# Last down product in other banks, output in three parts, router weights standing, modulation in one piece, squares first

## The chip, the cores and the metric

One core of a Trainium2 chip runs the whole program. The metric is device microseconds; less is better. TensorE (PE) multiplies, VectorE (DVE) and ScalarE (ACT) do elementwise work, SyncE (SP) issues nearly all DMA. TensorE's clock has two levels, 1.2 and 2.4 GHz; views give the granted one as a share of the higher.

## The reference, cut to what matters

Two transformer blocks, 256 tokens by 1024 channels, all in float32. The first has two layers, each with modulation from a conditioning vector `c`, a mixer of three attention kinds, and a feed-forward part, dense in layer 0 and a mixture of eight experts in layer 1.

```python
c_act = jax.nn.silu(c)
for layer in range(2):
    mod = c_act @ ada_w[layer] + ada_b[layer]
    sh1, sc1, g1, sh2, sc2, g2 = split(mod, 6)
    h = rms_norm(x, norm_mix[layer]) * (1.0 + sc1) + sh1
    x = x + g1 * mixer(h, ...)                 # begins with h @ w_in
    h = rms_norm(x, norm_ffn[layer]) * (1.0 + sc2) + sh2
    y = swiglu(h, ...) if layer == 0 else moe(h, ...)
    x = x + g2 * y
# moe: logits = h @ w_router (1024x8); top 2; softmax of the two; each expert's swiglu, weighted
# second block:
h = rms_norm(x, norm1_g); proj = h @ w_in_2    # z, xbc (4096 columns), dt, q, k, v, gates
x = x + merged(ssd, attention) @ w_out
u = causal_dwconv(rms_norm(x, norm2_g) @ w_up, ffn_conv_w, ffn_conv_b)
x = x + (silu(u_gate) * u_val) @ w_down        # 5632 columns up, 2816 rows down
```

## The kernel before, in words

All weights are packed on the host in one stream in the order of use, in slots of up to 2048 columns (1 MB). `plan()` lists the slots. SyncE loads them one by one into a ring of four (`load_to`); a slot's place is free when its last user (`last_use`) is done. A slot is one or two chunks of at most 1024 columns. Each chunk is split for TensorE: ScalarE copies the rounded high part to `whi` (`Scalar.split_to`, line 386), VectorE writes what remains to `wlo` (`Vector.split_to`, line 340). There are four pairs of buffers (`NS`), so ScalarE can be four chunks ahead of TensorE. A product of two split numbers is three matmuls (`mm3`, line 238). Transposes go through line 251. Each engine runs its own program written out in order (`tensor_program`, `scalar_program`, `vector_program`, `sync_program`) and waits on counters of the others' finished work; within an engine nothing is reordered, so a `split_to` put ahead of something makes it wait for that chunk.

*Start.* The first 2048 columns of layer 0's modulation (shift and scale of the first norm) come in four quarters of 512, each in two slots. For a quarter, TensorE multiplies half the rows on one partition (`pe_mods`), VectorE sums the other half (`dve_mods`), and TensorE turns both into columns with narrow matmuls (`pe_mods_turn`). The norm's factors `rs` are broadcast along the tokens (`pe_along`), ScalarE copies that (`act_root`), VectorE scales the transposed `x` block by block, ScalarE adds the shift and rounds to `hT`, VectorE makes `hTl` (`dve_mod_t`, `act_mod_t`; eight blocks, with weight splits put between them by `split_between`). Before, quarters 0 and 1 (in plan order the first halves of shift and scale) are followed by blocks 0 to 3 and half of the first projection `inA0`, and quarters 2 and 3 (`pe_second_half`, called at its third chunk) by the rest.

*Routing* (`pe_routing`, 1744). For each of eight blocks k, token columns of `hT` and `hTl` are the stationary operand and 8 router columns the moving one: six matmuls per block. Between them the blocks are turned back to rows (4 transposes each) for the later choice of tokens. The broadcast of the output gate `g3` (16 fp32 records) comes ahead of the ranks, which need VectorE's choice of the two best (`sel`), and the picks (`pe_pick`) need the ranks and `place`.

*Between the blocks.* After the last expert a branch skips the code for an overfull expert (`when_over`). ScalarE then splits the first two chunks of `xbc` (`a.split_to(... + 2)` in `squares`) and squares the rows of `x` (`act_squares`, `act_last_squares`); from the sums come `rs` and the norm, as above. `pe_cols` multiplies the first two blocks of `xbc` together, k by k, as the norm's blocks come.

*End.* `pe_second_ffn` makes 44 blocks of the up product in banks 0 to 3 of PSUM in turn, each read by the convolution on ScalarE and VectorE, then the down product in banks 0 to 3 (two token tiles by two column halves), in 11 slots. `pe_down` takes all four banks ahead of its first matmul. `dve_down` adds the result to `x` in four pieces, column half 0 first; the output is stored by one DMA after the last.

Of the kernel before, what the change touches and what calls it, by code (L numbers as in the profile page):

```python
# [15 lines left out]
KT = D // 128  # L16
# [69 lines left out]
def plan():  # L86
    p = ada(0, 0, 512) + ada(0, 1024, 1536)
    for l in range(2):
# [442 lines left out]
def pe_start(K, pe):  # L531

    pe_mods(K, pe, 0)
    pe_mods(K, pe, 1)
    pe_mods_turn(K, pe, 0)
    pe_mods_turn(K, pe, 1)
    pe_turn(K, pe, "nm0", lambda j, i: K.x[:, i, 128 * j:128 * j + 128], KT, "v")
    pe_along(K, pe, "nm0")
    pe_mods(K, pe, 2)


def pe_second_half(K, pe):

    pe_mods_turn(K, pe, 2)
    pe_mods(K, pe, 3)
    pe_mods_turn(K, pe, 3)
# [16 lines left out]
def dve_start(K, v):  # L563
# [34 lines left out]


# [159 lines left out]
def dve_mod_t(K, v, s, scale, shift=None, j0=0, j1=KT):  # L759
# [9 lines left out]
    for j in range(j0, j1):  # L769
# [469 lines left out]
def pe_mixer(K, pe, l):  # L1239
# [472 lines left out]
def dve_down(K, v, s, parts, gate, norm):  # L1712

    v.split_to(min(parts[-1] + NS - 1, K.fence(parts[-1])))
    for half in range(2):
        if half and norm:
            dve_eps(K, v, norm)
        for i in range(2):
# [5 lines left out]
            else:  # L1724
                v.tt(xs, K.ps[2 * i + half][:, :], xs, ALU.add, key=(s, "y", i, half))
# [18 lines left out]
def pe_routing(K, pe):  # L1744

    pe.take(0)
    block = ready(K, pe, "nf1")
    for k in range(KT):
        block(k)
        o = slice(8 * k, 8 * k + 8)  # L1750
        for i in range(2):
            pe.mm3(K.ps[0][:, 8 * i:8 * i + 8], hrows(K)(k, i), (K.rout[:, 0, o], K.rout[:, 1, o]), k == 0 and i == 0, k == KT - 1,
                   done="logits" if k == KT - 1 and i else None)
        for j in (k - 1, k) if k % 2 else ():
            for part, src in enumerate((K.hT, K.hTl)):
                for i in range(2):
                    b = BACK[part][i]
                    if j % 4 == 0:
                        pe.take(b)
                    pe.tr(K.ps[b][:, 128 * (j % 4):128 * (j % 4) + 128], src[:, j, 128 * i:128 * i + 128].bitcast(F32),  # L1760
# [1302 lines left out]
```

## Time and profile before

| | us |
|---|---|
| median of 3 runs | 2177.68 (2173.34 to 2182.85) |
| profiled execution, device time | 2185.45 |
| its span | 2183.7 |
| ScalarE busy | 1329.7 (61%) |
| DMA engines | 497.18 MB, mean 228 GB/s |
| mean granted clock of TensorE | 0.946 |

The span runs from the first to the last instruction. The order in it is: start and mixer 0 to 229, dense part, mixer 1 to 593, routing to 625, experts to 1423, second block to the end. A time in a row is counted from the span's start; `[a <-b]` says that the engine was idle for a and that b ended it. In a window's row each engine has its busy time and the number of its instructions, then follow the granted clock, the share of time that the DMA engines were busy, and their rate.

### The profile page before, as it was taken

The page shows a single profiled execution, that of the slowest core. Times are in us where ns is not written, and L with a number is a line of the kernel's source. Part 1 is how long each engine was busy: PE and PEld are TensorE (multiplying, and loading weights), DVE is VectorE, ACT ScalarE, POOL GpSimd, SP SyncE. Part 2 cuts the span into 40 slices and gives each one's busy share as a digit, 9 for nine tenths or more (in the row PEclk, how much of TensorE's full clock was granted, in tenths as well). Part 3 has the DMA queues.
Part 4 walks back from the last instruction along what each step waited for, and adds up shares of the span by engine and source line. Part 5 has one row for each costly group of instructions (what it writes and reads, how often), then busy time and mean ns, then how long its engine had stood idle before and what let it go on. Part 6 is the DMA issues. An engine that isn't in the chain of part 4 may idle for free. (4 is left out here: it accounts for less than half of the span.)

```text
span 2183.7 us, 28021 instructions
## 1 busy us (share of the span) xinstructions
PE 2012.0 (92%) x11093; PEld 1731.4 (79%) x11093; DVE 1671.3 (77%) x2155; ACT 1329.7 (61%) x1968; POOL 0.2 (0%) x4
## 2 busy tenths in 40 slices
PE   7878999987899999999999999979999988889999
PEld 4667778876788888888888887769877878878987
DVE  4877888677669989998998999768655655567873
ACT  2564543357568777787877786657556544536652
POOL 0000000000000000000000000000000000000000
PEclk8886999999889999999999999989999989889999
DMA  7615688741249989998998998655314532224542
GB/s 272 232 54 209 245 315 325 282 150 39 97 163 368 360 337 360 360 365 326 363 365 331 357 370 317 246 184 180 137 44 154 198 112 97 97 97 143 186 163 107
DMA packets 70089, 497.18 MB, mean 228 GB/s; under 512 B 8000, under 2 KB 8256, under 8 KB 10688
## 3 DMA queue, kind: packets, MB, share of 16 engines
q1 hardware_dynamic: 69664, 494.28, 61.6%
q8 instruction: 89, 1.46, 0.3%
q10 hardware_dynamic: 288, 1.05, 0.1%
q14 instruction: 48, 0.39, 0.1%
HBM read 494.25 MB, written 1.05 MB: 227 GB/s over the span
## 5 line engine op out<-in xcount | busy, mean ns | idle before, releaser
L340 DVE TENSOR_TENSOR wlo<-ring,whi 128x1024 fp32r<-128x1024 f32 (+1 forms) x845 | 1016.7, 1216 | 292.5 <-ACT whi L386 274.5
L386 ACT ACTIVATE whi<-ring 128x1024 fp32r<-128x1024 f32 (+1 forms) x845 | 886.2, 1054 | 525.9 <-PE ps L238 455.7
L238 PE MATMUL ps<-whi,hT 128*128 128x256 f32 (+2 forms) x944 | 325.2, 344 | 27.6 <-ACT wa L366 4.7
L238 PE MATMUL ps<-wlo,hT 128*128 128x256 f32 (+2 forms) x944 | 319.9, 339 | 0.0
L238 PE MATMUL ps<-whi,hTl 128*128 128x256 f32 (+2 forms) x944 | 319.4, 338 | 0.0
L238 PE MATMUL ps<-whi,xg 128*128 128x512 f32 (+1 forms) x768 | 290.5, 378 | 5.4 <-DVE wlo L340 5.2
L238 PE MATMUL ps<-whi,xgl 128*128 128x512 f32 (+1 forms) x768 | 286.6, 373 | 0.0
L238 PE MATMUL ps<-wlo,xg 128*128 128x512 f32 (+1 forms) x768 | 286.4, 373 | 0.0
L238 PEld LDWEIGHTS ps<-whi,hT 128*128 128x128 f32 x944 | 187.8, 199 | 52.4 <-issue 6.7
L238 PE MATMUL ps<-whi,hf 128*128 128x512 f32 x528 | 210.1, 398 | 11.2 <-DVE wlo L340 4.9
L238 PE MATMUL ps<-wlo,hf 128*128 128x512 f32 x528 | 207.6, 393 | 0.0
L238 PEld LDWEIGHTS ps<-whi,hTl 128*128 128x128 f32 x944 | 187.0, 198 | 17.6
L238 PEld LDWEIGHTS ps<-wlo,hT 128*128 128x128 f32 x944 | 187.4, 199 | 16.8
L238 PE MATMUL ps<-hT,whi 128*128 128x256 f32 (+1 forms) x616 | 176.3, 286 | 6.0 <-DVE hTl L287 4.0
L238 PE MATMUL ps<-hTl,whi 128*128 128x256 f32 (+1 forms) x616 | 175.6, 285 | 0.0
L238 PE MATMUL ps<-hT,wlo 128*128 128x256 f32 (+1 forms) x616 | 174.8, 284 | 0.0
L238 PEld LDWEIGHTS ps<-whi,xg 128*128 128x128 f32 x768 | 145.3, 189 | 31.2 <-DVE wlo L340 6.3
L238 PEld LDWEIGHTS ps<-whi,xgl 128*128 128x128 f32 x768 | 145.2, 189 | 25.9
L238 PEld LDWEIGHTS ps<-wlo,xg 128*128 128x128 f32 x768 | 145.4, 189 | 24.6
L238 PE MATMUL ps<-whi,hf1l 128*128 128x512 f32 x352 | 137.6, 391 | 0.0
L238 PEld LDWEIGHTS ps<-whi,hf 128*128 128x128 f32 x528 | 100.2, 190 | 32.5 <-DVE wlo L340 5.8
L238 PEld LDWEIGHTS ps<-hT,whi 128*128 128x128 f32 (+1 forms) x616 | 117.1, 190 | 7.0 <-ACT hT L366 4.8
(283 smaller groups left out, 2644.9 us busy)
## 6 DMA issues: line engine op xcount, KB each, us to landing
ring<-in_wstream SPq DMA_DIRECT2D x462, 1024.0 KB, 5.0
ring<-in_wstream SPq DMA_DIRECT2D x4, 832.0 KB, 6.2
ring<-in_wstream SPq DMA_DIRECT2D x6, 256.0 KB, 2.7
cst<-in_cst SPq DMA_DIRECT2D x1, 1028.0 KB, 7.6
x<-in_x SPq DMA_DIRECT2D x1, 1024.0 KB, 13.6
work<-in_bias ACTq DMA_DIRECT2D x2, 512.0 KB, 5.2
ring<-in_wstream SPq DMA_DIRECT2D x2, 512.0 KB, 3.9
out_x<-x SPq DMA_DIRECT2D x1, 1024.0 KB, 4.1
```

The source lines that it names most:

```text
L238: i = self.e.matmul(out, lhsT, rhs, start=start, stop=stop, skip_group_check=True)
L340: i = self.e.tensor_tensor(K.wlo[:, q % NS, 0:cols], src, hi.bitcast(F32), ALU.subtract)
L386: i = self.e.activation(K.whi[:, q % NS, 0:cols], K.ring[:, m % RING, at:at + cols], ACT.Copy)
```

## The change

The plan has the eight modulation slots first. The four quarters, with their turns and the transposes of `x`, are done in one run, the quarters in the order of their columns; the scale and all eight blocks of the norm follow, then the first projection without a break. In the routing the 8 router columns are stationary and 256 tokens move (three matmuls per block), the 8 rows of logits are copied by ScalarE and turned by two small transposes; the gate's second half is broadcast after the ranks. The splits ahead of the squares of `n1` are gone; chunks 1, 2 and 4 of `xbc` are split between the norm's blocks 2, 4 and 6. The last down product uses banks 4 to 7. The output goes in three DMAs, each behind its own addition.

```diff
 def plan():
-    p = ada(0, 0, 512) + ada(0, 1024, 1536)
+    p = ada(0, 0, 2048)
...
-                if (l, n, at) == (0, 0, 0):
-                    p += ada(0, 512, 1024) + ada(0, 1536, 2048)
...
 def pe_start(K, pe):
     pe_mods(K, pe, 0)
     pe_mods(K, pe, 1)
     pe_mods_turn(K, pe, 0)
+    pe_mods(K, pe, 2)
     pe_mods_turn(K, pe, 1)
     pe_turn(K, pe, "nm0", lambda j, i: K.x[:, i, 128 * j:128 * j + 128], KT, "v")
+    pe_mods(K, pe, 3)
+    pe_mods_turn(K, pe, 2)
     pe_along(K, pe, "nm0")
-    pe_mods(K, pe, 2)
-def pe_second_half(K, pe):
-    pe_mods_turn(K, pe, 2)
-    pe_mods(K, pe, 3)
     pe_mods_turn(K, pe, 3)
...
 def dve_start(K, v):
...
     dve_eps(K, v, "nm0")
+    dve_root(K, v, "nm0")
+    dve_mods(K, v, 2)
     dve_mods_turn(K, v, 1)
-    dve_root(K, v, "nm0")
-    v.split_to(1)
-    dve_mod_scale(K, v, 0, 0, "nm0", 0, 4)
-    dve_mod_t(K, v, "nm0", K.sc, shift_of(K, 0, 0), 0, 4)
-    dve_mods(K, v, 2)
     dve_mods(K, v, 3)
     dve_mods_turn(K, v, 2)
+    v.split_to(1)
     dve_mods_turn(K, v, 3)
-    dve_mod_scale(K, v, 0, 0, "nm0", 4, 8)
-    dve_mod_t(K, v, "nm0", K.sc, shift_of(K, 0, 0), 4, 8)
...
+BETWEEN = {"nm0": ("inA0", {2: 2, 4: 3, 6: 4}), "nf0": ("ffng", {4: 3, 6: 4}), "nm1": ("inA1", {4: 3, 6: 4}), "n1": ("xbc", {2: 1, 4: 2, 6: 4}),
+           "n2": ("up2", {4: 3, 6: 4})}
 def split_between(K, x, s, j):
-    stage = {"nm0": "inA0", "nf0": "ffng", "nm1": "inA1", "n1": "xbc", "n2": "up2"}.get(s)
-    if j == 2 and s == "nm0":
-        x.split_to(K.parts[stage][0] + 2)
-    if j in (4, 6) and stage:
-        x.split_to(K.parts[stage][0] + 1 + j // 2)
+    stage, parts = BETWEEN.get(s, (None, {}))
+    if j in parts:
+        x.split_to(K.parts[stage][0] + parts[j])
...
 def pe_routing(K, pe):
+    def back(j):
...
     for k in range(KT):
         block(k)
         o = slice(8 * k, 8 * k + 8)
-        for i in range(2):
-            pe.mm3(K.ps[0][:, 8 * i:8 * i + 8], hrows(K)(k, i), (K.rout[:, 0, o], K.rout[:, 1, o]), k == 0 and i == 0, k == KT - 1,
-                   done="logits" if k == KT - 1 and i else None)
-        for j in (k - 1, k) if k % 2 else ():
...
+        pe.mm3(K.ps[0][0:8, 0:256], (K.rout[:, 0, o], K.rout[:, 1, o]), (K.hT[:, k, :], K.hTl[:, k, :]), k == 0, k == KT - 1,
+               done="logit rows" if k == KT - 1 else None)
+        if k:
+            back(k - 1)
+    pe.wait_ge(K.act, "logit rows")
+    for i in range(2):
+        pe.tr(K.ps[0][:, 256 + 8 * i:264 + 8 * i], K.modrow[0:8, 0, 128 * i:128 * i + 128], done="logits" if i else None)
     pe.given(0, (K.dve, "logits"))
-    pe_broadcast(K, pe, "g3", (6, 7))
+    back(KT - 1)
+    pe_broadcast(K, pe, "g3", (6, 7), (0,))
...
     pe.given(2, (K.dve, "count"))
+    pe_broadcast(K, pe, "g3", (6, 7), (1,))
 def act_routing(K, a):
...
     for half in range(2):
+        if half:
+            a.wait_ge(K.pe, "logit rows")
+            a.act(K.modrow[0:8, 0, 0:256], K.ps[0][0:8, 0:256], ACT.Copy, key="logit rows", own=False)
...
     def squares(way):
         by = ("x", 7) if way else ("e", 7)
-        a.split_to(K.parts["xbc"][0] + 2)
...
 def pe_second_ffn(K, pe):
-    pe_down(K, pe, "f2", "down2", lambda k, i: pair(K.hf, k, i), 2, (0, 1, 2, 3), lambda k: ("f2", "lo", k))
+    pe_down(K, pe, "f2", "down2", lambda k, i: pair(K.hf, k, i), 2, (4, 5, 6, 7), lambda k: ("f2", "lo", k))
...
     dve_eps(K, v, "n1")
-    v.split_to(K.parts["xbc"][0] + 1)
     dve_root(K, v, "n1")
-    v.split_to(K.parts["xbc"][0] + 2)
     dve_mod_t(K, v, "n1", K.col("n1", 0, 8))
...
-    sp.wait_ge(K.dve, "end")
+    sp.wait_ge(K.dve, ("f2", "y", 1, 0))
     if sp.e is not None:
-        sp.e.dma_start(out, K.x[:, :, :]).then_inc(K.s_out.sem, 16)
-    sp.wait_ge(K.s_out, 16)
+        sp.e.dma_start(out[:, :, 0:512], K.x[:, :, 0:512]).then_inc(K.s_out.sem, 16)
+    for i in range(2):
+        sp.wait_ge(K.dve, ("f2", "y", i, 1))
+        if sp.e is not None:
+            sp.e.dma_start(out[:, i, 512:1024], K.x[:, i, 512:1024]).then_inc(K.s_out.sem, 16)
+    sp.wait_ge(K.s_out, 48)
```

## Rows read from the trace of the kernel before

**Rows 1.** the page's parts 1 and 5: busy us, count; a group's busy, mean ns

```profile
PE 2012.0 (92%) x11093; PEld 1731.4 (79%) x11093; DVE 1671.3 (77%) x2155; ACT 1329.7 (61%) x1968; POOL 0.2 (0%) x4
...
L340 DVE TENSOR_TENSOR wlo<-ring,whi 128x1024 fp32r<-128x1024 f32 (+1 forms) x845 | 1016.7, 1216 | 292.5 <-ACT whi L386 274.5
```

**Rows 2.** what the loading queue waited for: us in total, times, longest

```profile
SPq L415 <- DVE wlo L340: 1775.5, 419, 55.0
```

**Rows 3.** timeline ahead of the last down product: start us, us, engine, operation

```profile
2111.20 0.28 PE L238 MATMUL ps<-hT,wlo 128*128 128x256 f32 x1
...
2114.76 1.00 DVE L294 SCALAR_TENSOR_TENSOR ffn_w<-ps,cols,ffn_w 128x255 f32<-128x255 f32 x2
...
2116.01 0.77 PE L238 MATMUL ps<-whi,hf 128*128 128x512 f32 x1 [4.54 <-DVE ffn_w L294]
```

**Rows 4.** windows of the down product (engines' busy us, clock, DMA share, GB/s)

```profile
2116.00:2121.00 5.00, 4.99 (x12) 3.94 (x13) 0.71 (x2) 0.42 (x1) 0.00 (x0) 0.51 0.46 188
...
2121.10:2126.10 5.00, 5.00 (x23) 4.13 (x22) 2.17 (x2) 2.12 (x2) 0.00 (x0) 1.00 0.00 0
```

**Rows 5.** timeline of the store, SyncE's queue

```profile
2179.19 0.40 SPq L2758 DMA_DIRECT2D out_x<-x  x1
```

**Rows 6.** DMA issues: count, KB each, median us to landing

```profile
ring<-in_wstream SPq DMA_DIRECT2D x6, 256.0 KB, 2.7
...
out_x<-x SPq DMA_DIRECT2D x1, 1024.0 KB, 4.1
```

**Rows 7.** windows: routing on TensorE, and dense 256-column products at full clock

```profile
599.20:614.40 15.20, 15.20 (x73) 15.20 (x74) 5.06 (x13) 5.62 (x12) 0.00 (x0) 0.50 0.01 1
...
1448.00:1468.00 20.00, 20.00 (x169) 20.00 (x168) 17.45 (x29) 15.18 (x25) 0.00 (x0) 1.00 0.47 159
```

**Rows 8.** timeline of the routing: first read of the logits, ranks, picks

```profile
614.54 0.17 DVE L308 COPY rt<-ps 128x16 f32<-128x16 f32 x1 [10.09 <-PE ps L238]
...
619.20 0.70 PE L238 MATMUL ps<-sel,steps 128*128 128x8 f32 x5
...
621.05 0.72 PE L238 MATMUL ps<-place,rows_hi 128*128 128x256 f32 x4 [1.15 <-DVE count L308]
```

**Rows 9.** windows of a stretch with nothing but transposes on TensorE, and the next

```profile
1547.50:1550.60 3.10, 3.04 (x14) 2.67 (x15) 1.66 (x2) 1.09 (x3) 0.00 (x0) 0.50 0.31 61
...
1550.60:1552.00 1.40, 1.28 (x9) 0.89 (x8) 0.69 (x1) 0.60 (x1) 0.00 (x0) 0.89 1.03 433
```

**Rows 10.** timeline between the experts and the second block's first projection

```profile
1422.09 1.61 DVE L294 SCALAR_TENSOR_TENSOR x<-ps,rt,x 128x512 f32<-128x512 f32 x2 [1.28 <-PE ps L238]
...
1428.77 2.00 ACT L386 ACTIVATE whi<-ring 128x1024 fp32r<-128x1024 f32 x2 [18.63 <-DMA ring<-in_wstream]
...
1436.37 1.19 PE L238 MATMUL ps<-cst,rs 128*128 128x128 f32 x4 [8.78 <-DVE rs L294]
...
1447.12 0.36 PE L238 MATMUL ps<-hT,whi 128*128 128x256 f32 x1 [0.58 <-ACT hT L366]
```

**Rows 11.** windows of the start: turns, transposes, a quarter, the projection's second half

```profile
19.10:21.70 2.60, 2.55 (x16) 2.36 (x16) 0.91 (x2) 2.56 (x5) 0.00 (x0) 1.00 1.00 417
...
21.90:26.10 4.20, 4.15 (x17) 4.05 (x18) 0.17 (x1) 1.89 (x7) 0.00 (x0) 0.50 1.01 419
...
26.00:29.40 3.40, 3.40 (x17) 3.40 (x18) 0.97 (x6) 0.00 (x0) 0.00 (x0) 0.50 0.24 101
...
44.60:50.40 5.80, 5.80 (x9) 0.80 (x9) 0.00 (x0) 0.58 (x1) 0.00 (x0) 0.62 0.63 255
...
57.60:64.60 7.00, 7.00 (x25) 6.82 (x26) 5.29 (x8) 3.67 (x5) 0.00 (x0) 0.64 0.58 207
```

**Rows 12.** timeline of VectorE at the start: sums, second half of the scale loop

```profile
41.76 2.33 DVE L294 SCALAR_TENSOR_TENSOR gate<-ring,cact,gate 128x512 f32<-128x512 f32 x3
...
55.24 0.48 DVE L294 SCALAR_TENSOR_TENSOR aux<-ps,sc,cbm 128x256 f32<-128x256 f32 x1
...
60.41 0.49 DVE L294 SCALAR_TENSOR_TENSOR hTl<-aux,mod,hT 128x256 fp32r<-128x256 f32 x1 [0.19 <-ACT hT L368]
```

More of the change, by code:

```diff
@@ L746, in act_mod_t, with dve_mod_scale @@
             a.act(K.hT[:, j, :], K.rtmp4[:, j % 4, :], ACT.Identity, bias=shift[:, j:j + 1], key=(s, "hi", j), own=False)
-def dve_mod_scale(K, v, layer, which, gain, j0=0, j1=KT):
-    at = 8 * which + 8
-    v.stt(K.sc[:, j0:j1], K.mod[:, layer, at + j0:at + j1], 1.0, K.col(gain, j0, j1 - j0), ALU.add, ALU.mult)
+def dve_mod_scale(K, v, layer, which, gain):
+    v.stt(K.sc[:, :], K.mod[:, layer, 8 * which + 8:8 * which + 16], 1.0, K.col(gain, 0, 8), ALU.add, ALU.mult)
     v.last()
@@ L756, in shift_of, with dve_mod_t @@
     return K.mod[:, layer, 8 * which:8 * which + 8]
-def dve_mod_t(K, v, s, scale, shift=None, j0=0, j1=KT):
+def dve_mod_t(K, v, s, scale, shift=None):
     def low(j):
@@ L768, in dve_mod_t @@
     v.wait_ge(K.act, (s, "along"))
-    for j in range(j0, j1):
+    for j in range(KT):
         v.wait_ge(K.pe, (s, "t", j // 2 * 2))
@@ L774, in dve_mod_t @@
               key=(s, "v", j), own=False)
-        if j > j0:
+        if j:
             low(j - 1)
         split_between(K, v, s, j)
-    low(j1 - 1)
+    low(KT - 1)
 def pe_rows(K, pe, key, lhs, kt, banks=(0, 1, 2, 3), by=(("dve", 0), ("dve", 1)), block=None, at_part=None):
@@ L910, in dve_mods_turn, with pe_broadcast @@
 def dve_mods_turn(K, v, u):
-    at = (0, 8, 4, 12)[u]
     v.wait_ge(K.pe, ("modturn", u))
-    v.tt(K.mod[:, 0, at:at + 4], K.ps[COLUMN][:, 0:4], K.col("ab0", at, 4), ALU.add, key=("mods", u))
-def pe_broadcast(K, pe, s, banks):
-    for half in range(2):
+    v.tt(K.mod[:, 0, 4 * u:4 * u + 4], K.ps[COLUMN][:, 0:4], K.col("ab0", 4 * u, 4), ALU.add, key=("mods", u))
+def pe_broadcast(K, pe, s, banks, halves=(0, 1)):
+    for half in halves:
         b = banks[half]
@@ L1251, in values @@
         pe_values(K, pe, s, x, js[x])
-    pe_rows(K, pe, f"inA{l}", hrows(K), KT, by=COPIES, block=ready(K, pe, f"nm{l}"),
-            at_part=None if l else lambda n: pe_second_half(K, pe) if n == 2 else None)
+    pe_rows(K, pe, f"inA{l}", hrows(K), KT, by=COPIES, block=ready(K, pe, f"nm{l}"))
     pe_rows(K, pe, f"inD{l}", hrows(K), KT, by=COPIES, banks=BANKS_D)
@@ L1709, in dve_dense, with dve_down @@
     dve_down(K, v, "ff", parts, True, "nm1")
-def dve_down(K, v, s, parts, gate, norm):
+def dve_down(K, v, s, parts, gate, norm, bank=0):
     v.split_to(min(parts[-1] + NS - 1, K.fence(parts[-1])))
@@ L1724, in dve_down @@
             else:
-                v.tt(xs, K.ps[2 * i + half][:, :], xs, ALU.add, key=(s, "y", i, half))
+                v.tt(xs, K.ps[bank + 2 * i + half][:, :], xs, ALU.add, key=(s, "y", i, half))
 def act_down(K, a, parts, norm):
@@ L1744, in pe_routing @@
 def pe_routing(K, pe):
+    def back(j):
+        for part, src in enumerate((K.hT, K.hTl)):
+            for i in range(2):
+                b = BACK[part][i]
+                if j % 4 == 0:
+                    pe.take(b)
+                pe.tr(K.ps[b][:, 128 * (j % 4):128 * (j % 4) + 128], src[:, j, 128 * i:128 * i + 128].bitcast(F32),
+                      done=("back", j // 4, part, i) if j % 4 == 3 else None)
+                if j % 4 == 3:
+                    pe.given(b, (K.act, ("rows", j // 4, part, i)))
     pe.take(0)
@@ L1750, in pe_routing @@
         o = slice(8 * k, 8 * k + 8)
-        for i in range(2):
-            pe.mm3(K.ps[0][:, 8 * i:8 * i + 8], hrows(K)(k, i), (K.rout[:, 0, o], K.rout[:, 1, o]), k == 0 and i == 0, k == KT - 1,
-                   done="logits" if k == KT - 1 and i else None)
-        for j in (k - 1, k) if k % 2 else ():
[L1755 to L1760, printed above, removed]
-                          done=("back", j // 4, part, i) if j % 4 == 3 else None)
-                    if j % 4 == 3:
-                        pe.given(b, (K.act, ("rows", j // 4, part, i)))
+        pe.mm3(K.ps[0][0:8, 0:256], (K.rout[:, 0, o], K.rout[:, 1, o]), (K.hT[:, k, :], K.hTl[:, k, :]), k == 0, k == KT - 1,
[5 more added lines that the diff above has]
+        pe.tr(K.ps[0][:, 256 + 8 * i:264 + 8 * i], K.modrow[0:8, 0, 128 * i:128 * i + 128], done="logits" if i else None)
     pe.given(0, (K.dve, "logits"))
-    pe_broadcast(K, pe, "g3", (6, 7))
+    back(KT - 1)
+    pe_broadcast(K, pe, "g3", (6, 7), (0,))
     pe.take(2)
@@ L1800, in dve_routing @@
     v.wait_ge(K.pe, "logits")
-    v.copy(lg, K.ps[0][:, 0:16].rearrange("p (i e) -> p i e", i=2), key="logits")
+    v.copy(lg, K.ps[0][:, 256:272].rearrange("p (i e) -> p i e", i=2), key="logits")
     eidx = K.cst("eidx").unsqueeze(1).to_broadcast([128, 2, 8])
```

8 lines of the change are left out of this document (6 added, 2 removed).

## The prediction

> **What bounds the kernel now.** I read the page's busy shares first: TensorE is busy 92% of the span, VectorE's low split is the largest group beside it, 845 times 1.22 us [rows 1]. Then the loading queue's waits: its ring issue waits 419 times, 1775.5 us in all, for VectorE's low split, that is for room in the ring, so the loads are ahead of their use and DMA isn't the bound [rows 2]. What is left to win is where PE stands still or runs at half its clock: the start, the routing, the step from the experts to the second block, and the end. The timelines and windows of those places carry the rest.
>
> Profiled execution: span 2183.7, device time 2185.45 us; that is 7.8 above the median of the runs, 2177.68. I make the sum as a difference and take it off both.
>
> **1. Last down product in banks 4 to 7.** The up product's last matmul starts at 2111.20; the down product starts at 2116.01, after VectorE's last convolution taps (2114.76 + 1.00) free banks 0 to 3 [rows 3]. In the stop the clock fell: from 2116 12 matmuls take 5.00 us at 0.51 clock, later 22 to 23 take as much at 1.00 [rows 4], so 12 x (0.417 - 0.227) = 2.3 us more. Banks 4 to 7 hold nothing read after the last norm. The first chunk needs rows 0 of the hidden state, long split, and its weights: the splits run four chunks ahead, and the four that are ready give PE 4 x 12 x 0.227 = 10.9 us, to 2122.3. The fifth needs PE's release of the first (2114.1) and the last hidden rows off ScalarE and VectorE (about 2117), hence is split by about 2119: nothing is late next. Gain 4.81 - 0.24 (two steps of the old stream) + 2.3 = 6.9 us, bounds 6.3 and 7.2.
>
> **2. Output in three parts.** Now the store is issued at 2179.19, when the last add is done, and takes 4.1 us for 1 MB [rows 5, 6]. The last 256 KB now go alone; the first 512 KB start some 4.5 us and the second part 1.4 us earlier. The nearest row for 256 KB is a ring load's 2.7 us [rows 6]. Gain 4.1 - 2.7 = 1.4; bounds 0.5 (the parts queue up) and 2. SP's two more waits hold up nothing but the stores.
> The Trainium skill ("DMA: Bandwidth & Descriptors", Latency) puts a fixed cost of about 2 us on any transfer; by it nothing under 2 us is left of the 4.1, which agrees with the row.
>
> **3. Routing.** Now 48 matmuls of 8 columns and 28 transposes run from 599.2, 73 of them in 15.2 us at clock 0.50: 0.208 each, since each loads 128 columns of weights [rows 7]. The logits are read at 614.54, PE ranks at 619.20, picks at 621.05 [rows 8]. After: 24 matmuls with 8 weight columns and 256 moving ones (0.118 each at full clock, 169 in 20 us [rows 7], so 0.21 at half), and 28 transposes (the last four come behind the logits): 52 in all.
> All at half clock: 52 x 0.213 = 11.1, logit rows at 610.3; ScalarE's copy and two small transposes 1.3, logits at 611.6 instead of 614.54. From there to the ranks it was 4.66 but VectorE's chain is only 2.7 of it (half of the gate broadcast is now behind the ranks): ranks about 614.4, picks 1.85 later plus 0.4 for the second half broadcast: 616.6, gain 4.4.
> But this stream is full: every operation streams 256 cycles back to back, and such streams do raise the clock in this trace (below). It starts low; I let it rise about 5 us in, as at the start of the down product above (2116 to 2121 [rows 4]). Then 24 operations at 0.213 and 28 at 0.12: logit rows 607.7, ranks 612.1, picks 614.1, gain 7.0. PE then waits for VectorE about 1.5 us with little to do, which may cost the clock again: half of the 32 picks' difference, 1 us. I take 6; bounds 2 (half clock, and the picks too) and 8.5. Behind PE's new wait for ScalarE's copy stand only the two transposes, the last back-turn and the broadcast.
> The Trainium skill ("TensorE: Matmul & The Clock Gate", Part 4) says transposes don't count as busy for the clock gate, which would speak against me: 28 of the 52 are such. But here a stretch of nothing but fp32 transposes from 1547.5 runs at 0.50 and the clock is up in the next window, 0.89 [rows 9]. The trace disagrees; I go by it.
>
> **4. Squares first.** Now ScalarE splits two chunks ahead of the squares, and those wait 18.63 us for a load that lands at 1428.77, while x is final at 1423.7 (1422.09 + 1.61). So the rows' broadcast comes at 1436.37 [rows 10]. After: squares of the first half at 1419.5, of the second to 1425; root by 1426.5; broadcast when the transposes end, 1427.7; factors on VectorE from about 1429.8, 8 us earlier. Not all stays: both splits of the first two chunks now stand inside that loop (VectorE 4 x 1.22 in place of 2 x 1.22), and PE needs both chunks for its first product. Walking the loop (0.4 per VectorE step, 1.0 and 1.22 per split [rows 1, 10]) gives the second split at 1436.5 and the last low part at 1442.0. PE: 48 products from 1436.6, 5 us at half clock, then 0.12 each: ends 1444.6. Before, the last six of them started at 1447.12 [rows 10] and ended at 1447.9. Gain 3.2; bounds 0.5 (VectorE passes its branch late) and 5.
>
> **5. Modulation in one piece.** Now PE does two quarters of the modulation and half of the first projection, then two more quarters and the projection's second half, 57.6 to 64.6 [rows 11]. After, one run: quarter 2, turn 1, transposes of x, quarter 3, turn 2, broadcast, turn 3. A quarter took 5.8 at clock 0.62, so 3.6 at full and, as my estimate, 6.8 at half; a turn 2.6 at full or 4.2 at half, the transposes 3.4 at half [rows 11]. The loads run at 417 GB/s to about 27 [rows 11], 2.5 us a slot, so the slot of PE's third quarter is in at about 21.7, when PE is free; its 0.2 MB more than the w_in slot that stood there costs nothing more. From 21.7: quarter 5.3 (starts low), turn 2.9, transposes 3.4, quarter 4.6, turn 2.6, broadcast 0.5, turn 2.6: 43.6. VectorE's sums (2.33 + 0.5 = 2.8 each [rows 12]) run beside these. The w_in slots wait for ring places freed at 27 and land by 33, hidden; so do the other constants, queued behind one more slot. The scale loop then starts about 45, where now its second half starts at 55.24 and ends at 60.9 [rows 12]: 5.7 with two splits, so 2 x 5.7 - 1.0 = 10.4 for the whole. PE starts two steps in, at 46.9, and its 48 matmuls, 5 us at half clock (15) and 33 at 0.187, end 11.3 later: 58.2 against 64.6. (In the second half 25 took 7.0 at 0.64 [rows 11], 0.28 each, the mean of 0.345 and 0.187.) That is 6.4, and 5 is my value, one handover more being likely. Bounds: all at half clock, 21.7 + 6.8 + 4.2 + 3.4 + 6.8 + 4.2 + 1.1 + 4.2 = 52.4, end 65.6, a loss of 1; all at full, gain 8.
> The following projection's slots were waited for by none, and stay so.
>
> **Sum:** 6.9 + 1.4 + 6 + 3.2 + 5 = 22.5 us: 2163.0 for the profiled execution, 2155.2 for the median.
>
> **The rivals.**
> A, routing stays low: if turns don't raise the clock, step 3 gives 2 to 4.4, say 2.5: 2158.7. For it: the clock stood at 0.50 through 15 us of busy PE [rows 7]. Against: rows 9; and what ran then had 8 columns. 12%.
> B, the front's gains are given back: in the experts the stream of weights is nearly as fast as the loads can go, and if it were the bound, only steps 1, 2 and 4 (11.5) count: 2166.2. Against: the ring is full nearly always [rows 2]. 9%.
> C, squares first brings nothing, because VectorE comes out of its branch late, and the splits are in the loop: 19.3 left, 2158.4. 8%.
> D, slower than before: the start becomes a chain in which nothing overlaps. Per quarter 6.8 + 2.8 sums + 0.9 copy + 4.2 turn + 0.4, twice, and transposes and broadcast 4.5, splits 2, loop 10.4, then PE's 16.6 at half clock: 21.7 + 30.2 + 33.5 = 85.4, 21 us later than 64.6, against 17.5 won elsewhere: 2181. It decides from a first projection ending past 82 us. Against: VectorE's sums ran beside PE's quarters before. 4%.
> The forecast itself: 67%.
>
> **How the numbers follow.** Likeliest 2155.2. All lower bounds give a gain of 8.3, all upper ones 30.7; both at once are unlikely, and the runs of before spread by about 5 us each way. Range 2145 to 2168, which takes in A, B and C. About 0.5% (10.9 us) is what a measurement of this kernel can tell from no change: faster means under 2166.8. Nearly all of the forecast, A and C, and half of B lie there: 0.87; within 0.10; slower 0.03.
>
> **What would show it.** Down product: no stop between up2 and it, clock 1.00 through. Store: last transfer about 2.7 us. Routing: the first logits copy by 610 and the clock up before the picks. Squares: ScalarE's squares ahead of its splits, the row broadcast near 1428 (less what was won before). Start: first projection in one piece, over by about 58. Wrong would be: a DMA wait of PE's in the experts, a turn of the start at half clock throughout, a gap ahead of the fifth down chunk.

## The result, and the profile after

The changed kernel took 2156.38 us (median of 4 runs, 2151.98 to 2157.23) against 2176.48 for the kernel before beside it (4 runs, 2173.34 to 2182.85): ratio 0.9904, 95% interval 0.9882 to 0.9926. 2155.2 was forecast, with 2145 to 2168 as the range. Two more measurements of the same change, 5 rounds each, gave 0.9888 and 0.9889. The profiled execution after has a span of 2154.6 us, and 2156.47 with what lies around it, which is its median; the one before had 2183.7 and 2185.45, 9.0 above its median, so this pair of traces differs by 29.1 where the medians differ by 20.1. Every reading below is therefore taken inside a stretch, from one event to the next, and not from absolute times.

The page after, part 1, and its group of low splits; they answer to [rows 1]:

```profile
PE 2001.1 (93%) x11071; PEld 1718.9 (80%) x11071; DVE 1670.7 (78%) x2154; ACT 1329.6 (62%) x1969; POOL 0.2 (0%) x4
...
L338 DVE TENSOR_TENSOR wlo<-ring,whi 128x1024 fp32r<-128x1024 f32 (+1 forms) x845 | 1016.3, 1216 | 283.3 <-ACT whi L384 265.4
```

TensorE's work is nearly the same, 10.9 us less busy: what went are stops and time at the low clock. (L338 is the low split, L384 the high one, L236 a matmul, L249 a transpose; the kernel before has them two lines later.)

**The down product.** Timeline of TensorE where up ends and down begins, against [rows 3], and the windows against [rows 4] (busy us of PE, PEld, DVE, ACT, POOL, then the clock, DMA share, GB/s):

```profile
2091.28 0.28 PE L236 MATMUL ps<-hT,wlo 128*128 128x256 f32 x1
2091.41 0.39 PE L236 MATMUL ps<-whi,hf 128*128 128x512 f32 x1
```

```profile
2092.00:2097.00 5.00, 5.00 (x24) 4.11 (x23) 3.90 (x8) 2.60 (x5) 0.00 (x0) 1.00 0.48 151
2097.00:2102.00 5.00, 5.00 (x24) 4.14 (x23) 3.40 (x4) 2.50 (x3) 0.00 (x0) 1.00 0.48 152
```

The stop of 4.54 us is gone and the clock stays at 1.00, where it was 0.51; 24 matmuls run in 5 us from the first. No gap came ahead of the fifth chunk. From the start of the last up matmul to the start of the last add it was 67.27 us and is 60.20.

**The store.** Timeline of VectorE's last adds, of SyncE's queue, and the page's part on DMA issues, against [rows 5, 6]:

```profile
2151.49 0.69 DVE L285 TENSOR_TENSOR x<-ps,x 128x512 f32<-128x512 f32 x1 [0.67 <-PE ps L236]
```

```profile
2147.49 0.41 SPq L2757 DMA_DIRECT2D out_x<-x  x1
2150.84 1.69 SPq L2761 DMA_DIRECT2D out_x<-x  x2
```

```profile
out_x<-x SPq DMA_DIRECT2D x1, 512.0 KB, 2.8
...
out_x<-x SPq DMA_DIRECT2D x2, 256.0 KB, 2.0
```

The last 256 KB land in 2.0 us where 1 MB took 4.1; from the end of the last add to the end of the span it is 2.46 instead of 4.49. The Trainium skill ("DMA: Bandwidth & Descriptors", Latency and other measured facts) calls about 2 us the fixed part of a transfer. These stores lie under that: 2.0 us is the whole time of 256 KB, and as 1 MB took 4.1 and 512 KB 2.8, the part that does not grow with the size is, as an estimate from these two, 2.8 - 1.3 = 1.5 us.

**The routing.** Timeline of TensorE from the first router matmul, then windows, against [rows 7, 8]:

```profile
591.02 0.37 PE L236 MATMUL ps<-hT,rout 128*8 128x256 f32 x1 [2.15 <-DVE hTl L292]
...
598.87 0.33 PE L249 MATMUL ps<-cst,hTl 128*128 128x128 f32 x1 [0.16 <-ACT lowl L364]
...
600.80 0.28 PE L249 MATMUL ps<-cst,modrow 8*128 8x8 f32 x2
...
603.91 0.72 PE L236 MATMUL ps<-sel,steps 128*128 128x8 f32 x5 [1.34 <-DVE sel L285]
604.49 1.14 PE L236 MATMUL ps<-aux,cst 128*128 128x128 f32 x8
605.78 1.02 PE L236 MATMUL ps<-place,rows_hi 128*128 128x256 f32 x4 [0.16 <-DVE count L306]
```

```profile
591.00:594.00 3.00, 2.98 (x14) 2.05 (x15) 3.00 (x9) 1.86 (x4) 0.00 (x0) 0.50 0.00 0
594.00:597.00 3.00, 3.00 (x21) 2.62 (x20) 2.08 (x6) 1.84 (x6) 0.00 (x0) 0.71 0.00 0
597.00:600.00 3.00, 2.42 (x16) 1.43 (x15) 0.00 (x0) 1.81 (x4) 0.00 (x0) 1.00 0.00 0
600.00:603.00 3.00, 2.54 (x21) 2.06 (x19) 1.53 (x9) 1.99 (x5) 0.00 (x0) 1.00 0.03 8
603.00:606.00 3.00, 1.94 (x15) 1.77 (x16) 1.89 (x10) 0.45 (x1) 0.00 (x0) 1.00 0.00 0
606.00:609.00 3.00, 3.00 (x16) 3.00 (x16) 0.69 (x1) 1.05 (x2) 0.00 (x0) 0.50 0.00 0
```

The clock rises about 4.7 us into the stream of matmuls and transposes, where the old one stood at 0.50 for all its 15 us [rows 7]. The logits are read 10.2 us after the first router matmul instead of 15.3 and the picks start after 14.8 instead of 21.8. After TensorE's pause for VectorE the clock falls again and the first half of the picks runs at 0.50: the risk that the forecast priced at 1 us.

**The step to the second block.** Timelines of ScalarE, VectorE and TensorE, against [rows 10]:

```profile
1412.05 0.61 ACT L368 ACTIVATE xn<-x 128x512 f32<-128x512 f32 x1
...
1417.50 1.04 ACT L384 ACTIVATE whi<-ring 128x1024 fp32r<-128x1024 f32 x1
```

```profile
1409.70 1.61 DVE L292 SCALAR_TENSOR_TENSOR x<-ps,rt,x 128x512 f32<-128x512 f32 x2 [1.28 <-PE ps L236]
1411.64 0.17 DVE L277 TENSOR_SCALAR ssq<-ssq 128x2 f32<-128x2 f32 x1 [0.34 <-DVEq L456]
...
1427.35 0.99 DVE L285 TENSOR_TENSOR hTl<-aux,hT 128x256 fp32r<-128x256 f32 x2
```

```profile
1415.21 0.61 PE L236 MATMUL ps<-cst,rs 128*128 128x128 f32 x4
1423.21 0.55 PE L236 MATMUL ps<-hT,whi 128*128 128x256 f32 x1 [7.39 <-DVE wlo L338]
```

ScalarE's last square is done before its first split. VectorE's first instruction behind the branch waits 0.34 us, so it does not come out of it late. x is final at 1411.31: the broadcast comes 3.9 behind it (12.7 before), the first product 11.9 (15.9 before) and the first convolution tap (ScalarE's first read of a finished block), 21.0 (25.8 before).

**The start.** Windows of quarter 2, turn 1, transposes, quarter 3, turn 2, turn 3 and the projection, against [rows 11]; then VectorE's scale loop, against [rows 12]:

```profile
21.20:26.40 5.20, 5.19 (x9) 0.79 (x8) 3.13 (x10) 2.11 (x8) 0.00 (x0) 0.67 0.99 418
26.40:29.00 2.60, 2.60 (x18) 2.44 (x18) 1.34 (x2) 0.00 (x0) 0.00 (x0) 1.00 0.62 199
28.90:32.30 3.40, 3.40 (x18) 3.07 (x19) 2.90 (x5) 0.00 (x0) 0.00 (x0) 0.53 0.95 386
32.30:35.90 3.60, 3.60 (x9) 0.53 (x9) 0.00 (x0) 0.00 (x0) 0.00 (x0) 0.97 0.09 36
35.90:38.40 2.50, 2.50 (x18) 2.40 (x18) 0.68 (x1) 0.00 (x0) 0.00 (x0) 1.00 0.52 147
38.90:42.80 3.90, 3.89 (x17) 3.68 (x16) 1.02 (x1) 1.95 (x3) 0.00 (x0) 0.56 0.98 391
42.80:56.40 13.60, 11.48 (x50) 11.22 (x51) 12.13 (x23) 7.35 (x13) 0.00 (x0) 0.75 0.70 239
```

```profile
43.23 0.88 DVE L292 SCALAR_TENSOR_TENSOR aux<-ps,sc,cbm 128x256 f32<-128x256 f32 x2
...
53.04 0.48 DVE L292 SCALAR_TENSOR_TENSOR hTl<-aux,mod,hT 128x256 fp32r<-128x256 f32 x1 [0.19 <-ACT hT L366]
```

TensorE works without a stop from 21.2 to 42.8, the two quarters together in 9.0 us (9.9 were reckoned), and the loop takes 10.3 (10.4 reckoned).

### The profile page after: what moved, and what is told of

Same layout as the page of the kernel before. It is cut to its first block and busy times, and to the rows that moved or that the text cites. A ratio compares the mean times of both kernels' runs of the same rounds, so it can differ in the third digit from the quotient of the medians.

```text
span 2154.6 us, 27980 instructions
## 1 busy us (share of the span) xinstructions
PE 2001.1 (93%) x11071; PEld 1718.9 (80%) x11071; DVE 1670.7 (78%) x2154; ACT 1329.6 (62%) x1969; POOL 0.2 (0%) x4
## 5 line engine op out<-in xcount | busy, mean ns | idle before, releaser
L338 DVE TENSOR_TENSOR wlo<-ring,whi 128x1024 fp32r<-128x1024 f32 (+1 forms) x845 | 1016.3, 1216 | 283.3 <-ACT whi L384 265.4
L384 ACT ACTIVATE whi<-ring 128x1024 fp32r<-128x1024 f32 (+1 forms) x845 | 886.1, 1054 | 494.7 <-PE ps L236 447.5
L236 PE MATMUL ps<-whi,hT 128*128 128x256 f32 (+2 forms) x944 | 323.3, 343 | 26.9 <-DVE hTl L292 7.0
L236 PE MATMUL ps<-wlo,hT 128*128 128x256 f32 (+2 forms) x944 | 317.6, 336 | 0.0
L236 PE MATMUL ps<-whi,hTl 128*128 128x256 f32 (+2 forms) x944 | 317.0, 336 | 0.0
L236 PE MATMUL ps<-whi,xg 128*128 128x512 f32 (+1 forms) x768 | 290.6, 378 | 5.4 <-DVE wlo L338 5.2
L236 PE MATMUL ps<-whi,xgl 128*128 128x512 f32 (+1 forms) x768 | 286.8, 373 | 0.0
L236 PE MATMUL ps<-wlo,xg 128*128 128x512 f32 (+1 forms) x768 | 286.4, 373 | 0.0
L236 PEld LDWEIGHTS ps<-whi,hT 128*128 128x128 f32 x944 | 185.5, 196 | 51.4 <-issue 7.1
L236 PE MATMUL ps<-whi,hf 128*128 128x512 f32 x528 | 209.5, 397 | 6.5 <-DVE wlo L338 4.7
L236 PE MATMUL ps<-wlo,hf 128*128 128x512 f32 x528 | 206.9, 392 | 0.0
L236 PEld LDWEIGHTS ps<-wlo,hT 128*128 128x128 f32 x944 | 185.8, 197 | 16.6
L236 PEld LDWEIGHTS ps<-whi,hTl 128*128 128x128 f32 x944 | 185.0, 196 | 17.5
L236 PE MATMUL ps<-hT,whi 128*128 128x256 f32 (+1 forms) x616 | 176.2, 286 | 10.8 <-DVE wlo L338 7.4
L236 PE MATMUL ps<-hT,wlo 128*128 128x256 f32 (+1 forms) x616 | 175.6, 285 | 0.0
L236 PE MATMUL ps<-hTl,whi 128*128 128x256 f32 (+1 forms) x616 | 174.8, 284 | 0.0
L236 PEld LDWEIGHTS ps<-whi,xg 128*128 128x128 f32 x768 | 145.4, 189 | 31.2 <-DVE wlo L338 6.3
L236 PEld LDWEIGHTS ps<-whi,xgl 128*128 128x128 f32 x768 | 145.2, 189 | 25.9
L236 PEld LDWEIGHTS ps<-wlo,xg 128*128 128x128 f32 x768 | 145.5, 189 | 24.7
L236 PE MATMUL ps<-whi,hf1l 128*128 128x512 f32 x352 | 138.2, 393 | 0.0
L236 PEld LDWEIGHTS ps<-hT,whi 128*128 128x128 f32 (+1 forms) x616 | 117.1, 190 | 11.6 <-issue 9.7
L236 PEld LDWEIGHTS ps<-whi,hf 128*128 128x128 f32 x528 | 99.8, 189 | 27.4 <-DVE wlo L338 5.5
```

What stands on the lines that cost most here:

```text
L236: i = self.e.matmul(out, lhsT, rhs, start=start, stop=stop, skip_group_check=True)
L338: i = self.e.tensor_tensor(K.wlo[:, q % NS, 0:cols], src, hi.bitcast(F32), ALU.subtract)
L384: i = self.e.activation(K.whi[:, q % NS, 0:cols], K.ring[:, m % RING, at:at + cols], ACT.Copy)
```

## The experiments

Twelve runs of 5 rounds each, every ratio to the kernel before in the same call. "Start", "routing" and so on name the five parts. The columns give stretches of each profile, in us: from the span's start to the copy of the first projection; from the first router matmul to the first read of the logits, to the first gate and up product of the experts, and to the final x; from there to the first convolution tap; from the last up matmul to the last add; and from the end of that to the end of the span.

```
kernel          start: to first  first router  to first   to       x final to  last up    last add  ratio, 95% interval
                projection       to logits     gate-up    x final  first tap   to add     to end
before          64.7             15.3          26.1       824.5    25.8        67.3       4.49
before_again    60.8             15.3          26.1       824.1    25.8        67.3       4.50      0.9998 (0.9983-1.0012)
after           56.4             10.2          20.5       820.3    21.0        60.2       2.46      0.9904 (0.9882-0.9926)
after_again     53.9             10.7          19.5       818.0    20.9        60.2       2.48      0.9888 (0.9863-0.9913)
after_third     55.2             10.2          20.5       819.9    20.9        60.2       2.47      0.9889 (0.9871-0.9906)
start_only      56.3             15.3          26.2       824.2    25.7        67.0       4.5       0.9976 (0.9961-0.999)
routing_only    62.1             10.2          20.5       820.2    25.8        67.2       4.5       0.9972 (0.9956-0.9988)
down_only       58.3             15.3          25.3       822.4    25.9        60.2       4.5       0.9957 (0.9942-0.9972)
squares_only    60.9             15.3          26.0       823.8    19.9        67.2       4.5       0.9975 (0.9959-0.999)
store_only      61.9             15.3          26.1       824.4    25.9        67.3       2.5       0.9987 (0.9973-1.0001)
backs_last      53.0              6.8          18.1       815.4    21.4        60.2       2.46      0.9876 (0.9852-0.99)
pair_at_two     54.5             10.2          20.5       820.0    18.9        60.2       2.48      0.986  (0.9842-0.9878)
back_and_pair   54.8              6.8          18.1       816.0    18.6        60.2       2.47      0.9869 (0.9851-0.9887)
picks_padded    57.1             10.2          21.0       817.5    19.7        60.2       2.48      0.9889 (0.9872-0.9906)
```

**The two kernels again** (no edit), which give the noise that the others are read against.

> The kernel before, unchanged, traced a second time. Theory (the profiled execution of before at 2185.45 us had bad luck with TensorE's clock in stretches that the change doesn't touch): its trace is shorter than that, near 2177, and the difference lies in stretches with short stops, not in the five edited places, which take the same to 1 us. Rival (the edited places themselves vary by several us): the start, the routing or the step to the second block differs by over 2 us between the two traces.

> The changed kernel, unchanged, traced a second time. Theory: ratio to before 0.990 to 0.991; edited places as in the first trace: projection copied out at 56.4, routing from its first matmul to the picks 14.8 us, down product without a stop. Rival: the routing's clock falls or rises elsewhere and its length differs by 2 us or more.

Measured: before 2178.31 us (0.9998), after 2153.17 (0.9888). Two executions of the unchanged kernel before differ by 3.9 us in the first projection alone and by 7.3 in the span; the clock was low for 239 us in all in the one and for 222 in the other. So for the start the rival of the first text came true, and the second text missed as well: the changed kernel's projection was over at 53.9 instead of 56.4, and its gate and up product came 1.0 sooner, after picks at full clock. The three profiles of the changed kernel have spans of 2146.6 to 2157.5. A difference of less than some 11 us between two spans is no evidence, while the stretches that no such fall touches repeat to 0.1.

**One part each on the kernel before.** Start alone:

```diff
-    p = ada(0, 0, 512) + ada(0, 1024, 1536)
+    p = ada(0, 0, 2048)
...
+    pe_mods(K, pe, 2)
     pe_mods_turn(K, pe, 1)
...
```

> Before with the modulation in one piece alone. Theory (the gain of the start, 8.3 us in the traces, is carried to the end since nothing behind it is bound by loads): 5 to 9 us faster, ratio 0.996 to 0.998, and its trace has the first projection copied out at 56 to 58. Rival (given back by waits in the first mixer): the projection is earlier but the time within 1 us of before.

Measured: 2172.11 us, 0.9976. The first projection is over at 56.3. Over the 8 profiles with this part it is so at 55.1 in the mean, over the 6 without at 61.4: 6.3 us.

Routing alone:

```diff
-            pe.mm3(K.ps[0][:, 8 * i:8 * i + 8], hrows(K)(k, i), (K.rout[:, 0, o], K.rout[:, 1, o]), k == 0 and i == 0, k == KT - 1,
+        pe.mm3(K.ps[0][0:8, 0:256], (K.rout[:, 0, o], K.rout[:, 1, o]), (K.hT[:, k, :], K.hTl[:, k, :]), k == 0, k == KT - 1,
...
```

> Before with the standing router weights, the blocks turned back one behind, and the gate's second half behind the ranks, alone. Theory: 5.6 us faster, first router matmul to picks 14.8 us in place of 21.9, clock up during the stream that is over half transposes. Rival (transposes don't count as busy): the clock stays at half through the stream and 2 to 4.4 us are won.

Measured: 2172.7 us, 0.9972. The logits come 5.1 us sooner and the first gate and up product 5.6, but x is final only 3.9 sooner (of 824.1). The experiments below take this up.

Down alone:

```diff
-    pe_down(K, pe, "f2", "down2", lambda k, i: pair(K.hf, k, i), 2, (0, 1, 2, 3), lambda k: ("f2", "lo", k))
+    pe_down(K, pe, "f2", "down2", lambda k, i: pair(K.hf, k, i), 2, (4, 5, 6, 7), lambda k: ("f2", "lo", k))
...
```

> Before with the last down product in banks 4 to 7, alone. Theory: 7 us faster, ratio 0.9968, of it 4.6 the stop and 2.4 the clock. Rival (the stop only moves, to the fifth chunk): a stop of TensorE some 11 us into the down product, and under 4 us won.

Measured: 2171.94 us, 0.9957. The end from the last up matmul to the last add takes 60.2 as in the whole change: 7.1 us, which the other parts neither add to nor take from.

Squares alone:

```diff
-        a.split_to(K.parts["xbc"][0] + 2)
...
+BETWEEN = {"nm0": ("inA0", {2: 2, 4: 3, 6: 4}), "nf0": ("ffng", {4: 3, 6: 4}), "nm1": ("inA1", {4: 3, 6: 4}), "n1": ("xbc", {2: 1, 4: 2, 6: 4}),
...
```

> Before with the squares ahead of the splits, alone. Theory: 3 to 5 us faster; the row broadcast comes as soon as x is turned, but TensorE then waits for the two splits inside the norm's loop. Rival (it is bound by the first load of xbc, which lands 4.9 us after its issue): under 2 us.

Measured: 2174.19 us, 0.9975. The first tap comes 19.9 us behind the final x, instead of 25.8: 5.9, more than the 3 to 5 expected and 1.0 more than in the whole change. The first product comes at 11.9 in both; here the clock was back at full 14.9 us behind the final x, in the three profiles of the changed kernel at 17.3 to 17.4.

Store alone:

```diff
-        sp.e.dma_start(out, K.x[:, :, :]).then_inc(K.s_out.sem, 16)
+            sp.e.dma_start(out[:, :, 0:512], K.x[:, :, 0:512]).then_inc(K.s_out.sem, 16)
+    for i in range(2):
...
+            sp.e.dma_start(out[:, i, 512:1024], K.x[:, i, 512:1024]).then_inc(K.s_out.sem, 16)
```

> Before with the output in three DMAs, alone. Theory: from the last addition to the end 2.4 us in place of 4.5, so 2 us faster, which the timing can hardly tell. Rival (the three queue up behind one another): no gain.

Measured: 2176.66 us, 0.9987 (0.9973 to 1.0001): by the time alone this is not told from nothing; the timeline shows the 2.0 us.

The five gains by time add up to 0.0133, 29 us with some 7 either way; the whole gave 0.0096 to 0.0112, 21 to 24. The two are not told apart, so an interplay of a few us can't be excluded by the times. The stretches show two places where a gain shrinks: in the routing, taken up below, and the 1.0 us of the squares.

**The turns back behind the logits.** In the changed kernel four of the turns back (the transposes that give the hidden rows) wait for ScalarE in the middle of the router matmuls: they start at 597.41, 597.89, 598.38 and 598.87, 0.48 apart, where two such transposes together take 0.38 elsewhere at this clock. Nobody needs them before the picks. The edit moves them, and has ScalarE copy the logit rows first.

```diff
-        if k:
-            back(k - 1)
+    back(0)
     pe.wait_ge(K.act, "logit rows")
...
+    for j in range(1, 4):
+        back(j)
     pe_broadcast(K, pe, "g3", (6, 7), (0,))
...
+    for j in range(4, KT):
+        back(j)
...
-        if half:
+        if not half:
             a.wait_ge(K.pe, "logit rows")
...
```

> After, with the blocks' turning back to rows taken out of the router's loop: only block 0 is turned ahead of the logits, blocks 1 to 3 behind them, 4 to 7 behind the ranks. Theory (in the loop TensorE is late against VectorE because of the transposes): logits 3 to 4 us earlier, picks held by the row copies, 1 to 2.5 us won against after. It also tells the clock's rule: with 24 matmuls of 256 columns at VectorE's pace and hardly a transpose, the clock comes up if such columns alone do it. Rival (the stream without transposes isn't dense enough): the clock stays low until the transposes, and nothing is won.

Measured: 2153.58 us, 0.9876. The logits come after 6.8 us, the picks after 13.9 and the first gate and up product after 18.1, 2.4 us sooner than in the changed kernel, and x is final 4.5 sooner (815.4 of 820). By the time it is not told from the changed kernel. The windows answer the question about the clock:

```profile
593.30:596.30 3.00, 2.95 (x12) 1.01 (x12) 3.00 (x9) 1.82 (x4) 0.00 (x0) 0.50 0.00 0
596.30:600.10 3.80, 3.06 (x20) 1.67 (x20) 2.12 (x6) 2.11 (x6) 0.00 (x0) 0.97 0.00 0
```

It was up 3.1 us after the first router matmul (4.6 in back_and_pair below), before the first of the turns back. So the rise in the changed kernel's routing says nothing of its transposes.

**Both first chunks at block 2.** TensorE's first product waits for the low part of the second chunk.

```diff
-BETWEEN = {"nm0": ("inA0", {2: 2, 4: 3, 6: 4}), "nf0": ("ffng", {4: 3, 6: 4}), "nm1": ("inA1", {4: 3, 6: 4}), "n1": ("xbc", {2: 1, 4: 2, 6: 4}),
+BETWEEN = {"nm0": ("inA0", {2: 2, 4: 3, 6: 4}), "nf0": ("ffng", {4: 3, 6: 4}), "nm1": ("inA1", {4: 3, 6: 4}), "n1": ("xbc", {2: 2, 4: 3, 6: 4}),
```

> The changed kernel, but in the loop behind the experts both first chunks of the second block's convolution projection are split at block 2 (instead of one at 2 and one at 4; the four splits inside the loop stay four). In the changed kernel TensorE's first product starts 11.7 to 11.9 us behind the final x, when the low part of the second chunk is split. If the pair is what the start waits for: the second chunk is split one step of the loop earlier, the first product starts 1.5 to 2 us earlier (9.9 to 10.4 behind the final x), and then TensorE stops once for the last blocks of the loop, so that the first convolution tap comes 0.5 to 1.5 us earlier: ratio 0.9993 to 0.9998 of the changed kernel, not to be told from it by the time, only by the timeline. If the length of the loop decides (its last low part comes 16.5 us behind the final x in both): the first tap stays at 20.9, within 0.3. Slower by 0.5 or more if the two splits side by side keep the first blocks' scaling waiting on VectorE.

Measured: 2148.16 us, 0.986; timeline of TensorE:

```profile
1420.02 0.55 PE L236 MATMUL ps<-hT,whi 128*128 128x256 f32 x1 [5.48 <-DVE wlo L338]
```

That is 9.9 us behind the final x (11.7 to 11.9 before this edit): 1.8 to 2.0 sooner, so the pair was what the start waited for. The first tap comes at 18.9, 2.0 sooner, but not all of that is the edit's. The clock was back 13.9 us behind the final x here and at 17.3 to 17.4 in the changed kernel; in squares_only and picks_padded, which have the pair as the changed kernel has it, it was back at 14.8 to 14.9 and the tap came at 19.9 and 19.7. Against those the edit brings 0.9 to 1.0. The second stop that I had expected is there, and short:

```profile
1426.64 0.36 PE L236 MATMUL ps<-hT,whi 128*128 128x256 f32 x1 [0.30 <-ACT hT L364]
```

Here the end of the loop holds TensorE too; in back_and_pair, where the clock came back 0.8 later, it does not. The time lies 6.8 us under the changed kernel's in the same call, more than the timeline accounts for, with overlapping intervals.

**Both edits together.**

> Both order edits on the changed kernel: the turns back of the hidden rows stand behind the logits (but for the first), and both first chunks are split at block 2. The turns back last alone brought 0.9876 of the kernel before, the changed kernel 0.9888 and 0.9904, intervals overlapping. If both are worth what their timelines say (routing 2.4 us at the first gate and up product, the pair 0.5 to 1.5), this lies 2 to 4 us under the changed kernel: 0.9865 to 0.988 of the kernel before. If the time of the changed kernel is by now set by how long the clock stays low (190 to 215 us in its executions, which is worth up to 12 us), no difference shows: 0.988 to 0.990.

Measured: 2147.31 us, 0.9869. Both gains show in the stretches (18.1, and 18.6), and the time equals that of the pair alone. This and the one before have the lowest times of the study, some 7 us under the changed kernel beside them, though the intervals of the ratios overlap.

**Where the routing's gain went.** The distance from the first router matmul to the final x is 822.4 to 824.5 us without the routing part. With it the first gate and up product comes 5.6 us sooner and x is final 4 sooner. The windows of expert 7's last down product show the place; the kernel before (second measurement) and then the changed kernel:

```profile
1396.00:1399.00 3.00, 3.00 (x15) 2.47 (x14) 3.00 (x4) 2.25 (x3) 0.00 (x0) 1.00 0.73 309
1399.00:1402.00 3.00, 3.00 (x15) 2.49 (x14) 2.20 (x2) 2.40 (x3) 0.00 (x0) 1.00 0.01 3
...
1408.00:1411.00 3.00, 3.00 (x6) 1.19 (x4) 0.75 (x1) 0.00 (x0) 0.00 (x0) 0.56 0.00 0
```

```profile
1388.00:1391.00 3.00, 2.68 (x6) 2.15 (x7) 3.00 (x4) 0.00 (x0) 0.00 (x0) 0.50 0.51 153
1391.00:1394.00 3.00, 3.00 (x8) 2.31 (x7) 1.89 (x2) 1.15 (x2) 0.00 (x0) 0.50 0.47 199
...
1403.00:1406.00 3.00, 3.00 (x11) 1.92 (x11) 1.53 (x2) 0.00 (x0) 0.00 (x0) 1.00 0.00 0
```

Both come out of the same stop (TensorE waits 2.74 us for the low split before, 2.78 after). Before, TensorE goes on at full clock, 15 matmuls in 3 us, and the clock falls later; after, it is low for some 6.8 us from the restart. From VectorE's split of the product's second chunk to the final x it takes 24.3 us in place of 23.05. That is 1.2 of the 1.6 us that are missing; the rest is gone before the stop, and was not followed up. A kernel was made that only shifts this: the last picks repeated five times.

```diff
+        for rep in range(5 if g == ("g", 0) and f == 7 else 0):
...
+                    pe.mm(K.ps[b][:, 128 * n * jj:128 * n * (jj + 1)], rows_of(K, f % 2, i)[:, 128 * j:128 * j + 128],
...
```

> The changed kernel with 20 matmuls more behind the picks (the last four of them, 256 columns each, repeated five times into the same bank, so the result stays): at 0.12 each at full clock 2.4 us later into the experts, 4 us if the clock is low there. It asks where some 2 us of the routing's gain went, which were there at expert 7's last down product and gone at the final x. Theory, the clock: in all kernels with the routing edit the clock is low for 6.8 us from the start of that product, in all others it is full there, and low for about 3.4 us later; nothing else differs. If where it falls hangs on the phase in which the stop comes, a shift of 2.4 moves it: the low stretch becomes 3.4 or moves as in the kernel before, and the first router matmul to final x, 820.3 and 818.0 without the pad, gets only 0 to 1.5 longer. Rival, a fixed cost of the routing edit (more held back, the branch entered later): the low stretch stays 6.8 and the distance grows by the full 2.4. The time: 0 to 2.4 us over the changed kernel, 0.989 to 0.990 of the kernel before.

Measured: 2155.12 us, 0.9889. Windows of the same product in it:

```profile
1389.00:1392.00 3.00, 3.00 (x14) 2.42 (x14) 3.00 (x3) 1.11 (x2) 0.00 (x0) 1.00 0.66 218
1392.00:1395.00 3.00, 3.00 (x15) 2.49 (x14) 3.00 (x4) 2.40 (x3) 0.00 (x0) 1.00 0.32 134
```

The low stretch is gone from there; the product to the final x takes 23.1 us. The rival, a fixed cost of the edit in this product, is refuted, and back_and_pair says the same, with the routing edit and 23.0. But my theory's own number was off too. I had the experts begin 2.4 us later; the first gate and up product came 0.5 later, and x was final 2.3 us *sooner* than in the changed kernel of the same call (817.5 against 819.9; one other execution of it had 818.0), although TensorE does 20 matmuls more. Some of the reason lies before the added work: in that execution the picks ran at full clock, the first 16 in 2.0 us, where the changed kernel of the first measurement took 3.4 at 0.50. That part is not shown to be the padding's doing. What decides where the clock falls stays open: the kernel before in both profiles and the four with one other part all show the first pattern, and the three profiles of the changed kernel, pair_at_two and routing_only all show the second (in after_third with full clock between two low stretches of 3.4), whether the start is 6 us shorter or not.

**The changed kernel once more**, beside these three.

> The changed kernel unchanged, in one call with the others, so that these are compared with it on one chip. 0.988 to 0.991 of the kernel before, the bounds that its two measurements gave.

Measured: 2154.91 us, 0.9889.

## Why the prediction was right

The forecast was a sum of five steps, 22.5 us. The medians give 20.1, and with the repeats (ratios 0.9904, 0.9888, 0.9889 of about 2178) 21, 24 and 24. By stretches, each a difference of like events:

1. Down product, 6.9 forecast: 7.1. The stop, the clock and the bound by ready chunks came as said.
2. Store, 1.4 forecast: 2.0, at the upper bound. The term was mis-sized by its row: a 256 KB load of the ring took 2.7 us, a 256 KB store takes 2.0. Whether the traffic around the loads or the direction makes the difference no run tells.
3. Routing, 6 forecast: 5.6 at the first gate and up product (6.6 in one execution, in which the picks kept more of the clock), of which about 4.2 reach the final x (819.7 in the mean of five profiles against 823.9). The picks start 7.1 sooner, where 7.0 was reckoned; then the low clock at the picks costs 1.5 us (10.4 from the logits to the gate and up product, 8.8 in the execution without it), where I had put 1: half of the picks' difference is 1.5 by my own figures too. The clock rose, so rival A fell. I had let it rise counting the transposes in [rows 9], against the Trainium skill's sentence; backs_last shows that the router matmuls alone bring it up, so the forecast was right here on a ground that this stretch does not test. That some of the gain is lost again 780 us later to where the clock falls was in no case of mine.
4. Squares first, 3.2 forecast: 4.9. Broadcast 3.9 us behind the final x as forecast (4.0). The walked loop was too long: its last low part 17.0 behind the final x against 18.3, the first product 11.9 against 12.9; and before, the product pair ended 0.6 later than the row I took for its last. When the clock comes back moves this term by 1.0 (5.9 in squares_only). Rival C fell with the 0.34 us at VectorE's branch.
5. Modulation in one piece, 5 forecast (6.4 worked out): 6.3 in the mean. The 1.4 us I took off for one more handover was not needed: the chain from 21.2 to 42.8 has none. The two turns between quarters ran at full clock; quarter 2 ran low in part (0.67), the transposes of x and turn 3 nearly throughout (0.53 and 0.56), which for a turn I had named as a sign of being wrong; the term held all the same. The first pair of profiles shows 8.3, since before had its worst start of six there. The lower bound was added up wrongly: from 52.4 the steps of the forecast (14.6 us) lead to 67.0, not to 65.6.

Rival B, the front's gains given back in the experts, fell: low splits counted off against each other in the two traces stand 13.8 us apart behind the routing and still so up to expert 7's last down product. Rival D fell at 56 us against its 82.

The sum of the stretches is 6.3 + 4.2 + 4.9 + 7.1 + 2.0 = 24.5 us. It lies above the first measurement, inside its interval (16 to 26 us), and within the noise of the repeats. That it comes within 2 us of the forecast is in part luck: the start, the squares, the store and the down product were 3.8 us too low in sum, the routing 1.8 too high.

## What to carry to other kernels

A stop can cost more than its length: at the down product it was 4.7 us of standing still and, by the rest of the 7.1 won, 2.4 of restart at the low clock. Turning a narrow product round, so that 24 matmuls of 256 columns replace 48 of 8, took 5.1 us off 15.3. Judge a small edit by stretches between like events, not by the span: those repeated to 0.1 us, while spans of one kernel differed by up to 11. And for a loop that feeds an engine ask which of its steps the engine's first instruction waits for: moving one split forward by two blocks started it 1.8 us sooner, of which about 1 reached the first tap once the clock's part is taken out.

## What the hardware showed that I had not expected

The clock comes back over transposes too: in [rows 9] nothing else ran before it rose, and in eleven of the fourteen profiles there is such a stretch, low with nothing but transposes on TensorE and full behind them (15 of them from 1531.0 on in the changed kernel). The Trainium skill ("TensorE: Matmul & The Clock Gate", Part 4) says of its transpose mode that it does not engage the full clock; for the fp32 transposes of this kernel the traces disagree. Whether they run in that mode the records, which call them MATMUL, do not show.

In the routing, all six profiles with 8 moving columns show the clock low from before the first router matmul until 18.2 to 20.1 us behind it, though TensorE was busy without a stop for the first 15; all eight with 256 columns show it up after 2.8 to 6.0 us. The edit also takes 24 matmuls out, and nothing here separates the two.

The same kernel's clock was low for 190 us in one execution and 213 in two others, without any edit. With half of such time lost that is an estimated 11 us, and the spans differ by 8.0 and 10.9: more than any single part of this change brought.

One and the same stop of 2.8 us before expert 7's last down product left the clock up in eight of the fourteen profiles, down in five, and down a little later in one; in the one profile with 20 matmuls added 780 us earlier it stayed up, and x was final 2.3 us sooner with more to do. One execution can't say that the added work did it.
